# Moving the four low-part subtractions of the gates' input sums from VectorE to GpSimd

## What is computed

```python
proj = x @ w_in[l] + b_in[l]
glu_in, q, k, v, gate_logits = jnp.split(proj, splits, axis=-1)
y_conv = conv_branch(glu_in, w_dw[l], b_dw[l], ln_conv_g[l], ln_conv_b[l], w_conv_out[l])
y_attn = chunked_attention(heads(q), heads(k), heads(v), rel_bias[l]) @ w_attn_out[l]
g_conv, g_attn = jnp.split(jax.nn.sigmoid(gate_logits), N_BRANCHES, axis=-1)
mixed = (g_conv * y_conv + g_attn * y_attn) @ w_o[l] + b_o[l]
x = layer_norm(ALPHA * x + mixed, ln1_g[l], ln1_b[l])
x = layer_norm(ALPHA * x + grouped_moe(x, ...), ln2_g[l], ln2_b[l])
```

## Time and profile before

| | us |
|---|---|
| median of 3 runs | 1127.01 |
| lowest, highest | 1126.13, 1128.60 |
| the profiled execution | 1122.16 |
| its span, first to last instruction | 1120.4 |
| TensorE busy | 1079.3 (96%) |
| VectorE busy | 832.7 (74%) |
| ScalarE busy | 557.0 (50%) |
| GpSimd busy | 361.8 (32%) |

### The profile page before, as it was taken

The page is one execution under the profiler, slowest core; times in us unless marked ns, Lnnn a source line. Parts: engine busy times, 40 slices in busy tenths (PEclk is TensorE's granted clock), DMA queues, the critical chain, the costliest instruction groups (busy, mean ns, idle before and its releaser), DMA issues.

```text
span 1120.4 us, 17230 instructions
## 1 busy us (share of the span) xinstructions
PE 1079.3 (96%) x5487; PEld 895.3 (80%) x5488; DVE 832.7 (74%) x1195; ACT 557.0 (50%) x854; POOL 361.8 (32%) x317
## 2 busy tenths in 40 slices
PE   8998999999999999999999999899999999999984
PEld 7786888889888889788888888788888888888762
DVE  7999999995667766665775588888588646548766
ACT  6312333334476655645331224487487535548764
POOL 2533645354275864667000000024122121112120
PEclk9999999999999999999999999999999999999998
DMA  9898545453211010460740335888999876699966
GB/s 331 245 237 187 151 151 154 147 150 123 60 36 43 21 42 1 168 246 20 272 188 1 150 151 199 312 319 315 376 328 368 313 246 180 210 380 331 349 196 253
DMA packets 60938, 222.68 MB, mean 199 GB/s; under 512 B 9169, under 2 KB 9553, under 8 KB 56770
## 3 DMA queue, kind: packets, MB, share of 16 engines
q1 hardware_dynamic: 51602, 182.49, 43.9%
q0 software_dynamic: 9264, 39.27, 14.4%
HBM read 189.27 MB, written 49.30 MB: 213 GB/s over the span
## 4 chain that ended last, share of the span: by engine, by line
PE 80%; DVE 8%; DMA 4%; ACT 2%; issue 2%; POOL 2%; SPq 1%; ACTq 0%; DVEq 0%; POOLq 0%
PE ps L682 14%; PE ps L684 13%; PE ps L683 13%; PE ps L1817 10%; PE ps L1819 10%; PE ps L1818 10%; PE ps L804 2%; DMA raw<-in_wblk 2%; PE ps L790 2%; DMA dn_raw<-in_wexp 2%; PE ps L776 2%; DVE ps L1242 2%; PE ps L1898 2%; PE ps L1813 1%; PE ps L1925 1%
## 5 line engine op out<-in xcount | busy, mean ns | idle before, releaser
L1716 DVE TENSOR_TENSOR gu<-gu (+1 forms) x128 | 148.5, 1218 | 35.3 <-issue 20.9
L1242 DVE SCALAR_TENSOR_TENSOR ps<-u,dw_t,ps 128x1024 f32<-128x1024 f32 x116 | 149.1, 1285 | 2.4
L1817 PE MATMUL ps<-gu,xgh 128*128 x336 | 133.9, 398 | 3.4 <-DVE xgl L2215 2.1
L1710 ACT ACTIVATE gu<-gu (+1 forms) x128 | 124.1, 1047 | 21.3 <-DMA gu<-in_wexp 13.2
L1819 PE MATMUL ps<-gu,xgl 128*128 x336 | 131.9, 392 | 0.0
L1818 PE MATMUL ps<-gu,xgh 128*128 x336 | 131.5, 391 | 0.0
L596 POOL TENSOR_SCALAR pr<-pr,rinv 128x640 f32<-128x640 f32 (+4 forms) x64 | 95.2, 1500 | 77.7 <-DVE rinv L1401 77.5
L682 PE MATMUL ps<-xh,wh 128*128 128x512 f32 x256 | 103.2, 403 | 4.0 <-DVE u L1226 1.3
L683 PE MATMUL ps<-xl,wh 128*128 128x512 f32 x256 | 100.0, 391 | 0.0
L684 PE MATMUL ps<-xh,wl 128*128 128x512 f32 x256 | 99.9, 390 | 0.0
L646 POOL TENSOR_TENSOR ul<-uraw,uh 128x512 fp32r<-128x512 f32 x52 | 66.3, 1372 | 67.2 <-ACT uh L1027 67.2
(11 more groups left out here) (308 smaller groups left out, 2656.0 us busy)
## 6 DMA issues: line engine op xcount, KB each, us to landing
gu<-in_wexp SPq DMA_DIRECT2D x64, 1024.0 KB, 9.1
dn_raw<-in_wexp SPq DMA_DIRECT2D x16, 2048.0 KB, 10.0
raw<-in_wblk SPq DMA_DIRECT2D x36, 512.0 KB, 4.1
gate_weight_sums<-in_wblk POOLq DMA_DIRECT2D x48, 256.0 KB, 6.1
uraw<-gate_weight_sums SPq DMA_DIRECT2D x32, 256.0 KB, 2.9
gate_cols<-gst SPq DMA_DIRECT2D x32, 256.0 KB, 3.2
uraw<-in_wblk SPq DMA_DIRECT2D x24, 256.0 KB, 2.7
xf<-acc_rows SPq DMA_DIRECT2D x8, 512.5 KB, 8.2
```

What stands on the lines that cost most here:

```text
L1242: dve.scalar_tensor_tensor(out=so_far if k < CW - 1 else cv[:, j, :], in0=tap, scalar=w, in1=so_far, op0=ALU.mult, op1=ALU.add).then_inc(c ...
L1710: eng.activation(gu[:, par, k, 0, :], gu[:, par, k, 1, :].bitcast(F32), ACT.Copy).then_inc(gu_hi, 1)
L1716: eng.tensor_tensor(gu[:, par, k, 1, :], gu[:, par, k, 1, :].bitcast(F32), gu[:, par, k, 0, :], ALU.subtract).then_inc(gu_lo, 1)
L1817: pe.matmul(o, a_h, b_h, start=first, stop=False)
```

## The change

The four low parts t_low leave VectorE. GpSimd makes them, number i behind the issue of round i + 1. Its rounds 5 and 6, which were in front of all its unit subtractions, now stand behind those of units 4 and 9. On VectorE, four of the seven taps of each step now come before the step's `low` or `first_low`, three after it, where all seven came after it.

```diff
+LATE_ROUNDS = {4: 5, 9: 6}
...
+                def input_sum_low(i):
+                    pool.wait_ge(t_sum, 4)
+                    pool.wait_ge(x_hi, KC + i + 1)
+                    pool.tensor_tensor(t_low[i], t_raw[i], t_high[i], ALU.subtract).then_inc(x_lo, 1)
+
                 pool.wait_ge(x_hi, KC)
-                for r in range(KC // 2 + 3):
+                for r in range(KC // 2 + 1):
                     sums_round(r)
+                    if r:
+                        input_sum_low(r - 1)
                 pool.wait_ge(u_lo, FIRST_UNITS)
                 for m in range(FIRST_UNITS, N_UNITS):
                     unit_low(m)
+                    if m in LATE_ROUNDS:
+                        sums_round(LATE_ROUNDS[m])
...
                 low(3)
                 input_sums()
-                for i in range(4):
-                    dve.wait_ge(x_hi, KC + i + 1)
-                    dve.tensor_tensor(t_low[i], t_raw[i], t_high[i], ALU.subtract).then_inc(x_lo, 1)
                 low(4)
                 for n in range(2, B_V[0]):
                     if n % 2 == 0:
                         glu(n // 2 - 1)
+                    some_taps(TAPS_A_STEP // 2)
                     if n + 3 < B_V[0]:
                         low(n + 3)
...
-                    some_taps(TAPS_A_STEP - 1)
+                    some_taps(TAPS_A_STEP // 2 - 1)
                 glu(CB - 1)
```

## The result

The changed kernel takes 1131.16 us (median of 9 runs, 1127.31 to 1134.55), the kernel before 1125.25 beside it (median of 9). The ratio is 1.0052, 95% interval 1.0032 to 1.0072: slower by 0.5%, 5.9 us, where 2.8 us less was forecast, and above the range (1119.0 to 1126.5). The profiled execution took 1132.4 us, its span is 1130.6 us.

The account below looks back on a forecast made before the run. TensorE was taken as the bound, waiting for VectorE's glu(3). Without a hold 6.1 us would go, the hold costs 3.3, the clock's 1.3 stay lost: 2.8 off 1127.01 gives 1124.2 us, range 1119.0 to 1126.5.

Parts of the forecast that it names:

- What bounds the kernel: TensorE, busy for 96% of the 1120.4 us span; its 5.44 us wait at unit 2 is for VectorE's late glu(3).
- Removed: VectorE's four subtractions at L1322, 8.8 us, go; glu(0) 4.5 us earlier and the 1.29 us wait at block 3 gone.
- Added, size: Four GpSimd subtractions of 128x2048 behind the issue of rounds 1 to 4, 4.6 us each, bounds 4.4 and 9.2.
- Rival C: GpSimd's 128x2048 subtraction takes double, 9.2 us; unit 2 starts at 110.2, 1.8 us later: 1128.8 us; chance 5%.
- The step that failed: GpSimd's second and third subtractions, in idle stretches from 55.8 and 76.3, meet only taps and glus on VectorE: no hold.
- The hold that was forecast: first_low 2, at 95.8 on VectorE, is kept out by GpSimd's fourth subtraction until 99.3, costing 3.3 of 6.1 us.
- the sum for glu(3): On VectorE glu(3) starts at 104.2, after the held first_low 2, first_low 3 and three taps; unit 2 at 105.6.
- The late rounds: GpSimd's rounds 5 and 6 behind units 4 and 9: cost 0, with 7 us of cover.
- The clock: TensorE idles 4.0 us before unit 2, its clock falls again, so 1.3 us stay lost; no fall would win them.
- The rule of the Trainium skill: A two-SBUF-input VectorE instruction and a SBUF-reading GpSimd one exclude each other; the one that starts first keeps the other out.

## Why the prediction was wrong, point by point

- **What bounds the kernel** held: VectorE's lateness at glu(3) is what TensorE paid for, and the kernels' times follow the start of unit 2, but for the run with the taps put off. What the prediction didn't say is that GpSimd's late start lay right behind; that run shows it, with 8.2 us at unit 4.
- **Removed**: right. glu(0) was to start at 36.5 and did at 36.79, low(5) at 43.34 (43.0), low(6) at 53.62 (53.3), the wait at block 3 went.
- **Added, size**: right. 4.6 us was taken from two rows; the one that stands alone, in the run with two waits, takes 4.59, and the changed kernel's four take 4.62 to 4.74 from the end of the issue in front. The Trainium skill's 4497 ns for a tensor_tensor of 2048 elements (GPSIMD Engine Reference, elementwise side-by-side cycle accounting) is 0.1 to 0.2 below that. Rival C's double size did not come; the loss it named did, from another cause.
- **The step that failed** is the sentence that the second and third subtraction "have only taps and glus beside them". It placed the second from 55.8 on, behind the issue, and so low(6), at 53.3, ahead of it, and put that hold at nothing. The trace shows low(6) at 53.62 with 8.02 us instead of 1.22, until 61.64, and the run in which only that subtraction waits for low(6) has 1.22 again and is some 10 us faster. So a hold can take in an instruction that VectorE starts before GpSimd's work is due. That puts glu(1) at 65.4 instead of 58.3, adds 3.9 us of wait at block 5, and shifts VectorE by 6.8 us.
- **The hold that was forecast** came too, but on another pair: since VectorE was late, it was first_low 0, and not 2, that met the fourth subtraction, at 92.48 instead of 95.8, for 6.0 us and not 3.3. Where the first hold is taken away, the forecast one is measured at 3.7.
- So the sum for glu(3): 104.2 was forecast and 113.82 came, 9.6 us later. 6.8 are the first hold's and 2.7 what the second took more than forecast.
- **The late rounds** cost nothing, right. What the prediction didn't see is that with glu(3) early they are needed: without them unit 4 waits for GpSimd, as in the run with the taps put off.
- **The clock**: a fall was forecast behind the wait at unit 2. It came behind both waits and lasted longer, 1.4 us more than before at the end of the units. The choice between 5.44 us idle (it fell) and 2.35 (it didn't) went by the length of the wait, and length alone doesn't decide: at block 3, 2.00 us idle was followed by 0.50 in the run with the late rounds and 2.64 us by 1.00 in the run with the taps split.
- **The rule of the Trainium skill** was cited from SBUF — State Buffer, "Who interferes with whom", as "the one that starts first". That section says that whoever issues first gets the ports; "starts first" stands in the page's section "SBUF: two separate sides". I took it for the order of the work. low(6) was first by its row and by that order and was the one kept out, so here the measurement decides against that reading. When a queued GpSimd instruction was issued no row shows, and by issue alone the 512 and 8 queued columns should have held as well, if they were issued as early; they didn't. The section also says that a GpSimd instruction that only writes doesn't contend; the memset, beside 1.22 us of low(6), doesn't contradict it, but doesn't test it either, since 512 columns that read did as little.

The medians differ by 5.9 and the shift at unit 55 is 8.2 us. What gives back the other 2 us isn't settled: one profiled execution of each stands against medians of runs that spread by 7 us. Behind the convolution's mean the code is the same in all kernels here, and it takes 861.5 to 869.5 us in their profiled executions, so 2 us say little.

## What to carry to other kernels

Before work is moved from VectorE to GpSimd, list VectorE's instructions with two SBUF inputs and the stretches in which GpSimd has long reading work queued, not only running (here 1536 columns or more), and keep them apart by order or by a wait: one wait turned 0.5% slower into 0.3% faster, two into 0.75%. Cutting the GpSimd instruction didn't help as long as its pieces followed each other. Then ask whether the move is needed at all: two edits that moved no work between engines gained as much here. And where a wait is long, look who would be late next: a second one may lie under it, so that two edits must be judged together.

## What was new about the hardware

- A GpSimd subtraction of 1536 or 2048 columns that is queued behind the issue of DMA transfers kept a two-input VectorE subtraction out whose row began 0.3 (54.00 against 54.31, in the run with the subtractions alone) to 0.8 us before GpSimd's own: 7.1 to 8.2 us for 1.2 us of work. With 512 or 8 queued columns, or a memset of 2048 (1.8 us of work), it took 1.2 us.
- Four GpSimd subtractions of 512 columns in a row let VectorE in only after the third.
- Idle time of TensorE alone doesn't say whether its granted clock falls: 2.00 us was followed by 0.50, 2.64 us at the same place in another kernel by 1.00.
